# A two-block transformer stack on one core: the attention bias written to DRAM as single rows and copied there from ScalarE's queue, and every third attention pair a banded one

## The chip, the cores and the metric

The kernel runs on one core of one Trainium2 chip. The metric is the device time of one execution in microseconds (us). Before the change the median of three runs is 2673.74 us (2669.78 to 2679.16). The profile is of one further execution.

The engines are named as the profile names them: PE is TensorE's matmul, PEld its weight load, DVE is VectorE, ACT is ScalarE, POOL is GpSimd and SP is SyncE. SPq and ACTq are the queues from which SP and ACT issue DMAs. An engine takes its instructions strictly in order, and a DMA issue is one of them.

## What is computed

One sequence of 512 tokens of width 1024 goes through a first block of two layers and then a second block of two layers. The change touches only the first block. Each of its layers is, in short:

```python
h = rms_norm(x, g_pre)
a_q, a_kv, a_g, b_cq, b_ckv, b_kr, c_q, c_kv, z = split_cols(h @ w_in)
# 4 heads, each with three branches: compressed keys, all blocks, window 512
o_a = g[..., 0] * o_cmp + g[..., 1] * o_slc + g[..., 2] * o_win
# 4 heads of causal attention over up-projected queries and keys (96 wide)
o_b = causal_block_attention(q_full, k_full, v, (64 + 32) ** -0.5)
# 8 heads, window 128, with a sink logit in the softmax
o_c = banded_attention(c_q, c_k, c_v, 128, rel_bias[4:], sinks)
mixed = concatenate([o_a, o_b, o_c]) * silu(z)
x = x + rms_norm(mixed @ w_out, g_post)
```

The first four and the last eight heads add a relative bias to their logits: `rel_bias[head, t5_bucket(query - key)]`. It depends on the distance alone, so for a head it is one row over all distances, and a tile of 128 queries needs that row shifted by one position from partition to partition. `rel_bias` is the same in both layers. The second block (a pooling and gated-recurrence mixer between two feed-forward parts, per layer) is the larger part of the time, and its code is the same before and after.

## The kernel before

Everything is kept with 128 features on the partitions and 512 tokens in a row. A dense product is done in float32 by three passes on PE: each weight tile (128 x 1024, 512 KB) is split on DVE into a high part (`one_hi`) and the rest (`one_lo`), and so are the activations (`xh`, `xl`). The weight tiles of the first block come through `fetch_first` from SP's queue into a ring of four raw buffers. The next fetch into a buffer waits until its tile is split. Per layer there are 24 tiles of `w_in` (function `attend`, loop over `i` in `tensor`, line 1036) and 8 of `w_out` (`project_out`).

PE writes the products of `w_in` into six PSUM banks in turn. DVE evicts them (`evict`, line 779) and multiplies by `xrstd`, the reciprocal root of the mean square of x, which ACT makes (lines 702 and 705) once PE has summed the squares (line 1048). So tile 6 can't start before the first eviction. DVE does the split of tile i + 2 ahead of the evictions of round i, in one order written out by hand. At round 10 DVE reads `s1`, a block of small weights that ACT's queue fetches (line 699).

The bias is made at the start of layer 0. PE multiplies `rel` by a one-hot matrix `hot` after its first two weight tiles (`distance_rows`, line 556), DVE adds a mask (`mask_rows`, line 565), and the results are `vec` (4 x 1024, one row for each of the four heads) and `near` (8 x 384). Two DMAs on SP's queue, after the fetch of tile 7, write each row 128 times to DRAM (`store_bias`, line 526): `far_bias` is 4 x 128 x 1024 (2048 KB) and `near_bias` 8 x 128 x 384 (1536 KB). After the fetch of tile 11 two more DMAs on SP's queue wait for both stores and read the shifted tiles `biasA` and `biasC` back (`read_bias`, line 532).

The attention is a list of 48 pairs (`attention_pairs`, line 348). A pair is two heads of one kind for one block of 128 queries: 24 of the three branches (cmp, slc, win), then 8 causal ones (mla), then 16 banded ones (swa). A pair goes through five stages on four engines, and the engines work on different pairs at the same time. At step j:

- PE multiplies queries by keys for pair j (line 959), transposes the probabilities of pair j - 3 (line 973) and multiplies those of pair j - 4 by the values (line 987);
- DVE adds the bias to the logits and takes the maximum (line 825), takes the reciprocals of the sums of pair j - 1 (line 799), and makes a third of the copies of the transposed probabilities (line 839);
- ACT takes the exponentials and their sums (line 764) and makes the other copies (line 773);
- POOL scales the probabilities (lines 665 and 666), both heads of a pair, but only the first head where the pair has over two key blocks (DVE then does the second).

Each of the eight output tiles has one of two PSUM banks, in turn; DVE multiplies a finished one by silu(z) (line 812). ACT and POOL turn the finished tiles into `xh` and `xl` for `w_out` (lines 751 and 1129).

Of the kernel before, what the change touches and what calls it, by code (L numbers as in the profile page):

```python
# [459 lines left out]
class First:  # L460


    def __init__(self, kit, ctx):
# [19 lines left out]
        with ExitStack() as early:  # L483
# [26 lines left out]
def start_engines(kit, first):  # L510
# [21 lines left out]
    def read_bias(sp):  # L532

        sp.wait_ge(s["stored"], 32)
        for dst, name, sem, heads, w, n in ((kit.biasC, "near", "read_c", C_HEADS, NEAR_W, 256),
                                            (kit.biasA, "far", "read_a", A_HEADS, 2 * T, BIAS_W)):
# [18 lines left out]

    def distance_rows(pe):
        pe.wait_ge(s["loaded"], 80)
# [3 lines left out]
        pe.wait_ge(s["vec_made"], 1)  # L561
        pe.matmul(bank[5][0:C_HEADS, 0:NEAR_W], first.rel[:, A_HEADS:], first.hot[:, 256:256 + NEAR_W],
                  start=True, stop=True).then_inc(s["vec_mm"], 1)

    def mask_rows(v):
        v.wait_ge(s["loaded"], 80)
        for i in range(2):
# [4 lines left out]
        v.tensor_tensor(first.near[:], bank[5][0:C_HEADS, 0:NEAR_W], first.msk_near[:], ALU.add  # L572
                        ).then_inc(s["vec_made"], 1)

    return dict(sync=sync, store_bias=store_bias, read_bias=read_bias, scalar=scalar, vector=vector, tensor=tensor,
                distance_rows=distance_rows, mask_rows=mask_rows)


def attend(kit, first, l, begin):
# [99 lines left out]
    def sync(sp):  # L679
        for n in range(max(n0, RAW_RING), n0 + st.per_layer):  # L680
            sp.wait_ge(st.w_split, n + 1)
            fetch_first(sp, st, n)
# [4 lines left out]

    def scalar(a):
# [1773 lines left out]
```

## Time and profile before

| | us |
|---|---|
| median of three runs | 2673.74 |
| the profiled execution | 2676.89 |
| its span on the core | 2674.8 |
| PE busy in the span | 2472.3 (92%) |
| DVE busy | 1294.3 (48%) |
| ACT busy | 661.5 (25%) |
| POOL busy | 654.8 (24%) |

The busy shares are means over stages with different limits. The page's row of 40 slices shows PE at 7 tenths in the first slice and 0 in the second (66.87 us each), and at 7 to 9 in all others. In the second slice PE's granted clock is at 5 tenths. The span less the profiled execution's own time is 2.1 us, which lies outside all that is told here.

### The profile page before, as it was taken

To read this page: it belongs to the slowest core of one execution; us is meant where nothing else is said; L and a number is where in the kernel's file an instruction comes from. 1 tells how busy PE (TensorE), PEld (TensorE's weight loads), DVE (VectorE), ACT (ScalarE), POOL (GpSimd) and SP (SyncE) were. 2 spreads that over 40 slices of the span, in tenths; PEclk is the share of its full clock that TensorE was granted. 3 is DMA by queue.
4 is the path that set the end of the run, shared out by engine and by line. 5 is a ranking of instruction groups with operands and counts; after the bars stand their busy time and mean duration, and the time that the engine had idled before them with its cause. 6 is when DMAs were issued, how large, how long until landed. Compare 5 with 4: busy or idle time off the path is not lost. (4 is left out here: it accounts for less than half of the span.)

```text
span 2674.8 us, 35071 instructions
## 1 busy us (share of the span) xinstructions
PE 2472.3 (92%) x13238; PEld 1985.8 (74%) x13238; DVE 1294.3 (48%) x1920; ACT 661.5 (25%) x1329; POOL 654.8 (24%) x510
## 2 busy tenths in 40 slices
PE   7089999999789999999899999899999998999997
PEld 5066677866668888788688888788888787788886
DVE  4045656557453334586643334433343776533344
ACT  3001643037121110253321110311100643311101
POOL 1000561016333331200333321233311101433311
PEclk9589999999989999998999999999999998999999
DMA  5341013200033332221223232223322221223322
GB/s 166 56 139 47 17 48 126 86 25 17 16 117 98 98 109 93 71 98 41 79 87 101 94 117 92 64 94 98 107 98 83 95 65 56 79 95 101 111 99 78
DMA packets 58641, 224.79 MB, mean 84 GB/s; under 512 B 6392, under 2 KB 8576, under 8 KB 58276
## 3 DMA queue, kind: packets, MB, share of 16 engines
q1 hardware_dynamic: 57380, 215.49, 25.3%
q10 hardware_dynamic: 1152, 7.78, 0.8%
q8 instruction: 77, 1.26, 0.2%
q14 instruction: 32, 0.26, 0.0%
HBM read 217.47 MB, written 5.77 MB: 83 GB/s over the span
## 5 line engine op out<-in xcount | busy, mean ns | idle before, releaser
L172 DVE CAST two_hi<-two_raw 128x1024 fp32r<-128x1024 f32 (+1 forms) x292 | 219.8, 753 | 908.0 <-PE bank L241 896.5
L234 PE MATMUL bank<-xh,two_hi 128*128 128x512 f32 x1728 | 429.6, 391 | 0.0
L241 PE MATMUL bank<-xl,two_hi 128*128 128x512 f32 x1728 | 427.5, 389 | 0.0
L237 PE MATMUL bank<-xh,two_lo 128*128 128x512 f32 x1728 | 426.9, 389 | 0.0
L174 DVE TENSOR_TENSOR two_lo<-two_raw,two_hi 128x1024 fp32r<-128x1024 f32 (+1 forms) x292 | 401.0, 1373 | 10.0
L237 PEld LDWEIGHTS bank<-xh,two_lo 128*128 128x128 f32 x1728 | 324.3, 188 | 67.5
L241 PEld LDWEIGHTS bank<-xl,two_hi 128*128 128x128 f32 x1728 | 324.3, 188 | 67.4
L234 PEld LDWEIGHTS bank<-xh,two_hi 128*128 128x128 f32 x1728 | 323.0, 188 | 68.2 <-issue 1.1
L1579 POOL TENSOR_TENSOR up_hm<-up_sg,up_hm 128x512 f32<-128x512 f32 x88 | 197.6, 2245 | 556.4 <-ACT up_hm L1561 556.4
L449 PE MATMUL bank<-xh,one_hi 128*128 128x512 f32 x448 | 122.5, 418 | 81.0 <-DVE one_hi L172 81.0
L234 PE MATMUL bank<-hh,two_hi 128*128 128x512 f32 x704 | 171.8, 392 | 0.0
L172 DVE CAST one_hi<-one_raw 128x1024 fp32r<-128x1024 f32 x64 | 45.5, 710 | 260.6 <-PE bank L456 134.8
L241 PE MATMUL bank<-hl,two_hi 128*128 128x512 f32 x704 | 171.4, 390 | 0.0
L237 PE MATMUL bank<-hh,two_lo 128*128 128x512 f32 x704 | 170.0, 389 | 0.0
L449 PEld LDWEIGHTS bank<-xh,one_hi 128*128 128x128 f32 x448 | 88.0, 198 | 104.8 <-issue 86.0
L1561 ACT ACTIVATE up_hm<-bank 128x512 f32<-128x512 f32 x88 | 52.9, 601 | 416.5 <-PE bank L241 413.7
L665 POOL TENSOR_SCALAR lg_ring<-lg_ring,inv,gate 128x31 f32<-128x31 f32 (+4 forms) x80 | 45.0, 570 | 450.6 <-DVE inv L799 450.3
L234 PEld LDWEIGHTS bank<-hh,two_hi 128*128 128x128 f32 x704 | 132.1, 188 | 29.3 <-issue 1.9
L237 PEld LDWEIGHTS bank<-hh,two_lo 128*128 128x128 f32 x704 | 132.1, 188 | 27.5
L241 PEld LDWEIGHTS bank<-hl,two_hi 128*128 128x128 f32 x704 | 132.2, 188 | 27.3
L1582 POOL TENSOR_TENSOR hl<-up_hm,hh 128x512 f32 x88 | 115.1, 1308 | 83.7 <-ACT hh L1563 83.7
L453 PE MATMUL bank<-xh,one_lo 128*128 128x512 f32 x448 | 112.7, 394 | 0.0
(289 smaller groups left out, 2923.2 us busy)
## 6 DMA issues: line engine op xcount, KB each, us to landing
two_raw<-in_up SPq DMA_DIRECT2D x180, 512.0 KB, 3.4
two_raw<-in_down SPq DMA_DIRECT2D x64, 704.0 KB, 4.0
one_raw<-in_w_in SPq DMA_DIRECT2D x48, 512.0 KB, 3.5
two_raw<-in_w_in SPq DMA_DIRECT2D x40, 512.0 KB, 3.4
one_raw<-in_w_out SPq DMA_DIRECT2D x16, 512.0 KB, 3.4
two_raw<-in_w_out SPq DMA_DIRECT2D x16, 512.0 KB, 4.1
w<-in_w ACTq DMA_DIRECT2D x2, 2048.0 KB, 11.6
x<-in_x SPq DMA_DIRECT2D x4, 512.0 KB, 6.9
```

The source lines that it names most:

```text
L172: v.tensor_copy(st.hi[:, h, 0:w], st.raw[:, r, 0:w]).then_inc(st.hi_made, 1)
L174: v.tensor_tensor(st.lo[:, h, 0:w], st.raw[:, r, 0:w], st.hi[:, h, 0:w].bitcast(F32), ALU.subtract).then_inc(st.w_split, 1)
L234: pe.matmul(out[:], st.hi[:, slot, k * P:(k + 1) * P], xh[:, h * kp + k, :], start=h == 0 and k == 0, stop=False)
L237: pe.matmul(out[:], st.lo[:, slot, k * P:(k + 1) * P], xh[:, h * kp + k, :], start=False, stop=False)
L241: mm = pe.matmul(out[:], st.hi[:, slot, k * P:(k + 1) * P], xl[:, h * kp + k, :], start=False, stop=h == pieces - 1 and k == kp - 1)
L449: pe.matmul(out[:], st.hi[:, slot, w * P:(w + 1) * P], xh[:, k, :], start=k == 0, stop=False)
L453: pe.matmul(out[:], st.lo[:, slot, w * P:(w + 1) * P], xh[:, k, :], start=False, stop=False)
L665: return eng.tensor_scalar(row, row, inv[:, i, hh:hh + 1], gate[:, u["n"], b:b + 1], ALU.mult, ALU.mult)
L1561: a.activation(hm[:, f, :], bank[1][:], ACT.Copy).then_inc(s["out_taken"], 1)
L1579: g.tensor_tensor(hm[:, f, :], sg[:, f, :], hm[:, f, :], ALU.mult).then_inc(s["h_made"], 1)
L1582: g.tensor_tensor(hl[:, at, :].rearrange("p o t -> p (o t)"), hm[:, f, :], hh[:, at, :].rearrange("p o t -> p (o t)").bitcast(F32), ALU.su ...
```

## The change

It has two parts.

The bias: the four small inputs (`rel`, `hot`, `msk`, `msk_near`) are fetched first of all on SP's queue. The one-hot products become PE's first instructions and the mask DVE's first after its memsets, and the last of the three products goes to a bank of its own. SP's queue stores only `vec` and `near` themselves, as 4 and 8 rows, and then fetches `k1`, which had been among the first. ACT's queue then copies each row 128 times from DRAM to DRAM (`copy_bias`), ahead of its fetches of `s1` and `w1`, and reads the shifted tiles back (`read_bias`) after the last of the eight Silu of layer 0. The reads by DVE of `biasA` and `biasC` are the same.

The attention: the list of pairs is made of triples, two from the old list without the banded ones and then one banded pair. So two output tiles are open at a time, the banded tiles mostly in bank 7 and the others mostly in bank 4. The tiles finish in the order 4, 0, 5, 1, 6, 2, 3, 7, and `w_out` takes them in that order.

```diff
@@ attention_pairs
+    others, banded = [u for u in pairs if u["kind"] != "swa"], [u for u in pairs if u["kind"] == "swa"]
+    pairs = [u for k in range(len(banded)) for u in (others[2 * k], others[2 * k + 1], banded[k])]
@@
-N_NSA, N_MLA = 24, 8
 SPLIT_AT = (17, 20)
-TILES = (0, 1, 2, 3, 4, 5, 6, 7)
+TILES = (4, 0, 5, 1, 6, 2, 3, 7)
...
+OUT_BANKS = (7, 4, 7, 4, 7, 4, 4, 7)
@@ start_engines
     def sync(sp):
+        for dst, src in ((first.rel, "rel"), (first.hot, "hot"), (first.msk, "msk"), (first.msk_near, "msk_near")):
+            sp.dma_start(dst[:], d[src]).then_inc(s["loaded"], 16)
         sp.dma_start(kit.gains[:], d["gains"]).then_inc(s["gains_in"], 16)
...
-        for dst, src in ((first.rel, "rel"), (first.hot, "hot"), (first.msk, "msk"), (first.msk_near, "msk_near"),
-                         (kit.k1, "k1")):
-            sp.dma_start(dst[:], d[src]).then_inc(s["loaded"], 16)
         for n in (2, 3):
             fetch_first(sp, st, n)
-
-    def store_bias(sp):
         sp.wait_ge(s["vec_made"], 3)
-        sp.dma_start(d["far"], first.vec[0:A_HEADS].unsqueeze(1).to_broadcast([A_HEADS, P, 2 * T])
-                     ).then_inc(s["stored"], 16)
-        sp.dma_start(d["near"], first.near[:].unsqueeze(1).to_broadcast([C_HEADS, P, NEAR_W])).then_inc(s["stored"], 16)
...
+        sp.dma_start(d["far_row"], first.vec[:]).then_inc(s["stored"], 16)
+        sp.dma_start(d["near_row"], first.near[:]).then_inc(s["stored"], 16)
+        sp.dma_start(kit.k1[:], d["k1"]).then_inc(s["k1_in"], 16)
+
+    spread = (("near", "read_c", kit.biasC, C_HEADS, NEAR_W, 256), ("far", "read_a", kit.biasA, A_HEADS, 2 * T, BIAS_W))
+
+    def copy_bias(a):
+
+        a.wait_ge(s["stored"], 32)
+        for name, _, _, heads, w, _ in spread:
+            row = d[f"{name}_row"]
+            a.dma_start(d[name], bass.AP(row.tensor, row.offset, [[w, heads], [0, P], [1, w]])).then_inc(s["copied"], 16)
+
+    def read_bias(a):
+
+        a.wait_ge(s["copied"], 32)
+        for name, sem, dst, heads, w, n in spread:
             src = d[name]
...
+        mask_rows(v)
 
     def tensor(pe):
         pe.sem_inc(st.mm_done, HL_RING)
         pe.wait_ge(s["set"], 3)
-
-    def distance_rows(pe):
-        pe.wait_ge(s["loaded"], 80)
+        pe.wait_ge(s["loaded"], 64)
         for i in range(2):
             pe.matmul(bank[(5, 3)[i]][0:A_HEADS, :], first.rel[:, 0:A_HEADS], first.hot[:, i * T:(i + 1) * T],
                       start=True, stop=True).then_inc(s["vec_mm"], 1)
-        pe.wait_ge(s["vec_made"], 1)
-        pe.matmul(bank[5][0:C_HEADS, 0:NEAR_W], first.rel[:, A_HEADS:], first.hot[:, 256:256 + NEAR_W],
+        pe.matmul(bank[7][0:C_HEADS, 0:NEAR_W], first.rel[:, A_HEADS:], first.hot[:, 256:256 + NEAR_W],
                   start=True, stop=True).then_inc(s["vec_mm"], 1)
@@ attend: sync
-            if n == 7:
-                begin["store_bias"](sp)
-            if n == 11:
-                begin["read_bias"](sp)
@@ attend: scalar
+        if l == 0:
+            begin["copy_bias"](a)
         a.dma_start(s1[:], d["s1"][l]).then_inc(s["s1_in"], 16)
         a.dma_start(w1[:], d["w1"][l]).then_inc(s["w1_in"], 16)
...
             a.activation(proj[:, C_Z + c, :], proj[:, C_Z + c, :], ACT.Silu).then_inc(s["z_made"], 1)
+            if l == 0 and c == DC - 1:
+                begin["read_bias"](a)
...
-        convert_at = {NU - 4: (0, 1), NU - 3: (2, 3), NU - 2: (4,), NU: (5,), NU + 1: (6,)}
+        convert_at = {}
+        for p in range(DC - 1):
+            at = max(NU - L_RING + p // 2 + TURN_LAG + 1, last_of[TILES[p]] + WEIGH_LAG + 2, *convert_at)
+            convert_at.setdefault(at, []).append(p)
@@ attend: vector, step
-                if x == NU - 1 or pairs[x + 1]["tile"] != pairs[x]["tile"]:
-                    tile = pairs[x]["tile"]
+                tile = pairs[x]["tile"]
+                if x == last_of[tile]:
@@ attend: tensor, weigh
-            order = TILES.index(tile)
-            if order >= 2:
-                pe.wait_ge(s["mixed"], order - 1)
+            ahead = [p for p in range(TILES.index(tile)) if OUT_BANKS[p] == out_bank[tile]]
+            if ahead:
+                pe.wait_ge(s["mixed"], ahead[-1] + 1)
```

What stands on SP's queue around the stores before; "waits" names the semaphore that holds an instruction back:

```order
L345 DMA one_raw<-in_w_in 128x1024 [waits one_w_split] x4
L528 DMA far_bias<-vec 512x1x1024 [waits start_vec_made]
L530 DMA near_bias<-near 1024x1x384
L345 DMA one_raw<-in_w_in 128x1024 [waits one_w_split] x4
L538 DMA biasC<-near_bias 128x8x256 [waits start_stored]
L538 DMA biasA<-far_bias 128x4x896
L345 DMA one_raw<-in_w_in 128x1024 [waits one_w_split] x12
```

And now, on the same queue:

```order
L521 DMA x<-in_x 128x1024 x2
L345 DMA one_raw<-in_w_in 128x1024 x2
L527 DMA far_bias_row<-vec 4x1024 [waits start_vec_made]
L528 DMA near_bias_row<-near 8x384
L529 DMA k<-in_k 128x1281
L345 DMA one_raw<-in_w_in 128x1024 [waits one_w_split] x20
```

The two wide stores and the two reads have left the queue of the weight fetches; two stores of 4 and 8 rows and the fetch of `k1` stand there instead, before tile 4.

What stands on ACT between the squares of x and the first Silu before (`s` is `s1`, `w` is `w1`, `proj` holds the projections):

```order
L698 ACTIVATE proj<-x 128x512 x8
L699 DMA s<-in_s 128x1835
L700 DMA w<-in_w 128x4096
L702 ACTIVATE xrstd<-bank,eps 128x512 [waits first0_xsq_summed]
L705 ACTIVATE xrstd<-xrstd 128x512 [waits first0_ln_made]
```

And now, on to the reads:

```order
L702 ACTIVATE proj<-x 128x512 x8
L538 DMA near_bias<-near_bias_row 1024x1x384 [waits start_stored]
L538 DMA far_bias<-far_bias_row 512x1x1024
L705 DMA s<-in_s 128x1835
L706 DMA w<-in_w 128x4096
L708 ACTIVATE xrstd<-bank,eps 128x512 [waits first0_xsq_summed]
L711 ACTIVATE xrstd<-xrstd 128x512 [waits first0_ln_made]
L712 ACT_TABLE_LOAD
L715 ACTIVATE proj<-proj 128x512 [waits first0_taken] x8
L545 DMA biasC<-near_bias 128x8x256 [waits start_copied]
L545 DMA biasA<-far_bias 128x4x896
```

The two copies now stand ahead of `s1`, `w1` and the two steps that make `xrstd`, and they wait for the row stores.

What POOL scales at the end of the causal pairs and in the banded ones before (`lg_ring` holds the probabilities, `inv` the reciprocals; 128x256 and 128x128 here are one head of a banded pair, 128x512 and 128x384 of a causal one):

```order
L666 TENSOR_SCALAR lg_ring<-lg_ring,inv 128x512
L666 TENSOR_SCALAR lg_ring<-lg_ring,inv 128x384
L666 TENSOR_SCALAR lg_ring<-lg_ring,inv 128x256 x2
L666 TENSOR_SCALAR lg_ring<-lg_ring,inv 128x128 x2
L666 TENSOR_SCALAR lg_ring<-lg_ring,inv 128x256 x6
```

And now, from the first pair on (lines with `gate` are the pairs of the three branches):

```order
L673 TENSOR_SCALAR lg_ring<-lg_ring,inv,gate 128x31 x2
L673 TENSOR_SCALAR lg_ring<-lg_ring,inv,gate 128x512
L674 TENSOR_SCALAR lg_ring<-lg_ring,inv 128x256 x2
L673 TENSOR_SCALAR lg_ring<-lg_ring,inv,gate 128x512
L673 TENSOR_SCALAR lg_ring<-lg_ring,inv,gate 128x31 x2
L674 TENSOR_SCALAR lg_ring<-lg_ring,inv 128x256 x2
```

The banded pairs no longer stand in one run at the end; each has two other pairs before it.

## Rows read from the trace of the kernel before

**Rows 1.** Timeline at PE's long wait: start, duration, engine, instruction, [idle before <-releaser].

```profile
62.81 1.97 PE L456 MATMUL bank<-xl,one_hi 128*128 128x512 f32 x8
...
144.92 0.69 DVE L172 CAST one_hi<-one_raw 128x1024 fp32r<-128x1024 f32 x1 [88.36 <-DMA one_raw<-in_w_in]
...
145.76 3.75 PE L449 MATMUL bank<-xh,one_hi 128*128 128x512 f32 x8 [80.98 <-DVE one_hi L172]
...
152.87 1.77 PEld L449 LDWEIGHTS bank<-xh,one_hi 128*128 128x128 f32 x8
```

**Rows 2.** Timeline of SP's queue, 30 to 144 us.

```profile
30.00 0.78 SPq L528 DMA_DIRECT2D far_bias<-vec  x1
30.82 34.25 SPq L530 DMA_DIRECT2D near_bias<-near  x1
...
65.11 56.72 SPq L345 DMA_DIRECT2D one_raw<-in_w_in  x1
...
143.66 0.39 SPq L538 DMA_DIRECT2D biasC<-near_bias  x1
```

**Rows 3.** DMA view, 40 to 50 us: the queue's packets, MB, share of 16 engines.

```profile
q1 hardware_dynamic: 64, 0.26, 24.5%
```

**Rows 4.** DMA view, 65 to 80 us.

```profile
q1 hardware_dynamic: 335, 0.76, 45.7%
```

**Rows 5.** DMA view, 2660 to 2675 us, the final store of x from 128 partitions.

```profile
GB/s 0 0 0 0 0 0 0 0 0 0 0 0 0 339 415 404 240 0 164 415 404 404 11 0 0 0 426 415 393 164 0 0 0 262 426 415 295 0 0 0
```

**Rows 6.** Timeline of PE around the one-hot products.

```profile
25.53 1.88 PE L559 MATMUL bank<-hot,rel 32*4 32x512 f32 x4
...
29.31 3.14 PE L449 MATMUL bank<-xh,one_hi 128*128 128x512 f32 x8
...
36.51 1.98 PE L449 MATMUL bank<-xh,one_hi 128*128 128x512 f32 x8
38.33 1.98 PE L453 MATMUL bank<-xh,one_lo 128*128 128x512 f32 x8
```

**Rows 7.** Timeline of the first 7 us: the small fetches and the first split.

```profile
4.33 0.74 SPq L522 DMA_DIRECT2D rel<-in_rel  x1
...
6.10 0.27 SPq L522 DMA_DIRECT2D msk_near<-in_msk_near  x1
...
6.67 0.69 DVE L172 CAST one_hi<-one_raw 128x1024 fp32r<-128x1024 f32 x1 [5.49 <-DMA one_raw<-in_w_in]
```

**Rows 8.** Busy time by stretch: us, PE, PEld, DVE, ACT, POOL (instructions), PEclk, DMA share, GB/s.

```profile
0.00:20.00 20.00, 7.67 (x25) 5.79 (x26) 6.98 (x7) 15.49 (x25) 12.89 (x12) 1.00 0.90 323
80.00:100.00 20.00, 0.00 (x0) 0.00 (x0) 0.00 (x0) 0.00 (x0) 0.00 (x0) 0.50 0.42 46
```

**Rows 9.** Timeline: xrstd on ACT, and DVE's first use of s1.

```profile
43.01 0.69 ACT L702 ACTIVATE xrstd<-bank,eps 128x512 f32<-128x512 f32 x1 [23.05 <-PE bank L1048]
...
166.72 0.16 DVE L875 TENSOR_SCALAR nsink<-s 128x8 f32<-128x8 f32 x1
```

**Rows 10.** Layer 0's attention by stretch (columns of rows 8).

```profile
263.19:309.87 46.68, 42.47 (x357) 25.89 (x356) 32.16 (x142) 31.77 (x115) 21.60 (x38) 0.97 0.07 24
309.87:328.30 18.43, 18.36 (x131) 12.15 (x130) 13.44 (x51) 12.09 (x39) 11.86 (x12) 1.00 0.01 2
328.30:354.60 26.30, 25.70 (x234) 16.21 (x233) 20.04 (x100) 20.38 (x70) 23.45 (x30) 1.00 0.01 2
354.60:362.50 7.90, 6.09 (x47) 4.03 (x47) 2.26 (x8) 5.34 (x16) 7.88 (x9) 0.78 0.00 0
```

**Rows 11.** POOL's groups by form, 328 to 359 us: count, busy, mean ns, idle before.

```profile
L666 POOL TENSOR_SCALAR lg_ring<-lg_ring,inv 128x256 f32<-128x256 f32 x25 | 22.8, 925 | 2.1 <-DVE inv L799 2.0
L666 POOL TENSOR_SCALAR lg_ring<-lg_ring,inv 128x128 f32<-128x128 f32 x10 | 5.9, 606 | 0.8 <-DVE inv L799 0.8
```

**Rows 12.** DVE's reads of the maxima (one for each head), layer 0 and layer 1.

```profile
L825 DVE DVE_READ_ACCUMULATOR2_ANT negm<- x96: 71/83/86, 263.3 to 355.2; 128x1 f32 x96
...
L825 DVE DVE_READ_ACCUMULATOR2_ANT negm<- x96: 71/83/86, 577.7 to 669.1; 128x1 f32 x96
```

More of the change, by code:

```diff
@@ L519, in sync @@
                 fetch_first(sp, st, i)
-        for dst, src in ((first.rel, "rel"), (first.hot, "hot"), (first.msk, "msk"), (first.msk_near, "msk_near"),
-                         (kit.k1, "k1")):
-            sp.dma_start(dst[:], d[src]).then_inc(s["loaded"], 16)
         for n in (2, 3):
             fetch_first(sp, st, n)
-    def store_bias(sp):
         sp.wait_ge(s["vec_made"], 3)
-        sp.dma_start(d["far"], first.vec[0:A_HEADS].unsqueeze(1).to_broadcast([A_HEADS, P, 2 * T])
-                     ).then_inc(s["stored"], 16)
-        sp.dma_start(d["near"], first.near[:].unsqueeze(1).to_broadcast([C_HEADS, P, NEAR_W])).then_inc(s["stored"], 16)
[L532 to L536, printed above, removed]
+        sp.dma_start(d["far_row"], first.vec[:]).then_inc(s["stored"], 16)
[10 more added lines that the diff above has]
+        for name, sem, dst, heads, w, n in spread:
             src = d[name]
-            sp.dma_start(dst[:], bass.AP(src.tensor, src.offset + P - 1, [[w - 1, P], [w * P, heads], [1, n]])
-                         ).then_inc(s[sem], 16)
+            a.dma_start(dst[:], bass.AP(src.tensor, src.offset + P - 1, [[w - 1, P], [w * P, heads], [1, n]])
+                        ).then_inc(s[sem], 16)
     def scalar(a):
@@ L571, in mask_rows @@
         v.wait_ge(s["vec_mm"], 3)
-        v.tensor_tensor(first.near[:], bank[5][0:C_HEADS, 0:NEAR_W], first.msk_near[:], ALU.add
+        v.tensor_tensor(first.near[:], bank[7][0:C_HEADS, 0:NEAR_W], first.msk_near[:], ALU.add
                         ).then_inc(s["vec_made"], 1)
-    return dict(sync=sync, store_bias=store_bias, read_bias=read_bias, scalar=scalar, vector=vector, tensor=tensor,
-                distance_rows=distance_rows, mask_rows=mask_rows)
+    return dict(sync=sync, copy_bias=copy_bias, read_bias=read_bias, scalar=scalar, vector=vector, tensor=tensor)
 def attend(kit, first, l, begin):
@@ L606, in attend @@
     turn_bank = [(3, 6)[g % 2] for g in range(len(groups))]
-    out_bank = {t: (4, 7)[i % 2] for i, t in enumerate(TILES)}
+    out_bank = {t: OUT_BANKS[i] for i, t in enumerate(TILES)}
+    last_of = {u["tile"]: i for i, u in enumerate(pairs)}
+    first_of = {kind: min(i for i, u in enumerate(pairs) if u["kind"] == kind) for kind in ("cmp", "mla", "swa")}
+    n_swa = [sum(u["kind"] == "swa" for u in pairs[:i + 1]) for i in range(NU)]
+    assert list(TILES) == sorted(TILES, key=last_of.get)
     def here(j):
@@ L773, in scalar @@
                         a.activation(dst, src, ACT.Copy).then_inc(s["pt_by_a"], 1)
-            for p in convert_at.get(j, ()):
+            for p in convert_at.pop(j, ()):
+                convert(p)
+        for late in convert_at.values():
+            for p in late:
                 convert(p)
@@ L880, in vector @@
                     v.wait_ge(start["stored"], 32)
+                    v.wait_ge(start["k1_in"], 16)
                 v.tensor_tensor(rot_k[:, 0, :], proj[64:96, C_KR, :], cos, ALU.mult).then_inc(s["rot_made"], 1)
@@ L934, in vector @@
         v.wait_ge(s["z_made"], DC)
-        v.wait_ge(start["read_a"], 16)
         for j in range(NU + WEIGH_LAG + 1):
-            if j == N_NSA + N_MLA:
+            if j == first_of["cmp"]:
+                v.wait_ge(start["read_a"], 16)
+            if j == first_of["swa"]:
                 v.wait_ge(start["read_c"], 16)
@@ L995, in step @@
                     pe.wait_ge(s["logits"], 2 * (i - 1))
[L996 to L998 removed]
+                if i == first_of["mla"]:
                     pe.wait_ge(s["qk_made"], 2 * B_HEADS)
                     pe.wait_ge(s["uk_kept"], B_HEADS)
+                if i == first_of["cmp"]:
+                    pe.wait_ge(s["kc_made"], 2)
                 for hh in range(2):
@@ L1050, in tensor @@
             if i == 12:
+                if l == 0:
+                    pe.wait_ge(start["k1_in"], 16)
                 pe.wait_ge(s["taken"], C_KR + 1)
@@ L2446, in program @@
     dram["far"] = nc.dram_tensor("far_bias", (A_HEADS, P, 2 * T), F32, kind="Internal").ap()
+    for kind, heads, w in (("far", A_HEADS, 2 * T), ("near", C_HEADS, NEAR_W)):
+        dram[f"{kind}_row"] = nc.dram_tensor(f"{kind}_bias_row", (heads, w), F32, kind="Internal").ap()
     dram["near"] = nc.dram_tensor("near_bias", (C_HEADS, P, NEAR_W), F32, kind="Internal").ap()
```

15 lines of the change are left out of this document (4 added, 11 removed).

## Prediction, made before the changed kernel ran

> **What bounds the kernel now.** I read the page's slices first: PE is the busiest engine everywhere, except that slice 2 of 40 shows it idle. The timeline of that slice shows one hole. PE ends a tile of `w_in` (tile 7) at about 64.4 us and starts tile 8 at 145.7 [rows 1]. The row names the split as its releaser, and the split's own row names the DMA of the weights, for which DVE had idled 88.36 us. Then I read SP's queue backwards [rows 2]: the fetch of tile 8 was issued at 65.11, because the issue of the `near` store before it had taken 34.25 us; its own issue took 56.72 us, and the queue's next step that waits for both stores passed at 143.66. So two stores of 3.5 MB hold the weight stream for 81 us. Elsewhere in the first block PE is nearly dense, except in the attention: there PE, DVE, ACT and POOL all have gaps, and in the banded stretch POOL is busy 23.45 of 26.30 us, in the tail after the last logits 7.88 of 7.90 [rows 10].
>
> **Why the stores are slow.** From 40 to 50 us the queue moves 0.26 MB with a 24.5% share of 16 DMA engines: four engines, all their time, 26 GB/s together [rows 3]. Once `near` runs beside it, 45.7%, so between seven and eight engines, and 51 GB/s [rows 4]. At the end of the kernel the same kind of transfer, SBUF to DRAM, but from 128 partitions, moves up to 426 GB/s [rows 5], 26.6 GB/s an engine. So writing DRAM isn't what is slow; four engines read four partitions at the pace of one. Two things could do that: few engines, and a shared way out of few partitions. The change takes away only the second, since its copies have the same shape (4 or 8 rows, each 128 times).
>
> **The bias, step by step.**
>
> *The hole.* PE idles 81.0 us [rows 1]. After it a tile takes 152.87 - 145.73 = 7.14 us; a steady one takes 3 x (38.33 - 36.51) = 5.46 [rows 6]. That is 1.7 us of lower clock. Both go, 82.7 us, if tiles 8 and on are fetched in time. In that case SP's queue holds nothing but fetches, which have four buffers of 5.46 us each ahead.
>
> *The one-hot products leave the middle.* PE leaves the dense products at 25.5 and returns at 29.31, and the tile after it again takes 36.51 - 29.31 = 7.20 us. Without both, tile 3 starts at 25.5 + 5.5 = 31.0 in place of 36.5: 5.5 us gained.
>
> *They come first instead.* Four issues on SP's queue, from 4.33 to 6.37 us [rows 7], 2.0 us, now stand ahead of x and the weights, so the first split moves from 6.67 to about 8.7. PE's products and DVE's masks take from 25.5 to about 30.0 in the old place, with 1.2 us of waiting for a shared bank; now they would start near 4.7, when the small inputs have landed, and DVE would be through near 8.2, under the wait for the first weights. I cost them at the 2.0 us of the queue; if the small inputs land 1 us later, 1 us more. Net of the start: 3.5 us gained.
>
> *The copies.* The row stores come behind 4 MB of x and weights. The first 20 us move 323 GB/s [rows 8], so I put their landing at 17 us. At 26.6 GB/s an engine, `far` is 128 x 4096 bytes on each of four engines, 19.7 us, and `near` 128 x 1536 on each of eight, 7.4 us. Together they end at 17 + 27 = 44 us. The bias is first read in the attention, at about 175 us, and the reads themselves (2.8 MB, behind the last Silu) pass beside the dense products as they did before. So the copies cost nothing by themselves. No row shows a copy from DRAM to DRAM; its bounds are 426 GB/s (all engines, 8 us) and the old pace (26 to 51 GB/s, 105 us). I take the pace of an engine from rows 5.
>
> *What waits behind them on ACT.* ACT is an engine here: an issue that doesn't return holds the step after it. In rows 2 the third transfer's issue returned only when much of the one before was through (34.25 of the 79 us that `far` takes at 26 GB/s, 0.43). By that, ACT is free of its issues at 17 + 7.4 + 0.43 x 19.7 = 33 us. It needs to be free when PE has the sum of squares, 43.01 [rows 9] less 3.5, so at 39.5. Six us to spare, and some 6 more before PE, which has six banks, would stop. `s1` lands behind the copies near 50; DVE reads it at 166.72 - 86 = 81. Nothing is added.
>
> Sum for the bias: 82.7 + 3.5 = 86.2 us.
>
> The Trainium skill has a rule against this part (DMA: Bandwidth & Descriptors, Why a DMA increments its semaphore by 16 and not by 1): a DMA uses the largest number of engines up to 16 that divides the slowest dimension of both sides, so these copies still run on 4 and 8. The trace agrees for the stores (24.5% and 45.7% of 16 engines). A reader who expects 16 engines would have the copies end at 25 us, not 44; the sum is the same by both.
>
> **The attention.** The work is the same: 48 pairs, the same operations, and DVE's share of the copies is 8448 columns for 8576. What moves is when. Layer 0 takes 99.3 us: 24 pairs of branches at 1.95 us each, 8 causal at 2.30, 16 banded at 1.64, and a tail of 7.9 [rows 10]. In the banded stretch POOL's need is 24 x 0.925 + 8 x 0.606 = 27.0 us [rows 11] for a stretch of 26.3, and what is left over runs on into the tail. Spread over all 48 pairs POOL has 61 us in 91. What is late next: in the banded stretch PE shows 25.70 busy of 26.30, DVE and ACT 20.0 and 20.4. PE's ends are modelled, so its true need lies between PEld's 16.2 and that 25.7. If a banded pair goes at 1.5 us instead of 1.64, that is 2.3 us; and the tail, with POOL's backlog gone and the clock not at 0.78, may give 1.7. I take 4 us a layer. Far ends: banded pairs at the pace of DVE and ACT (1.27), the tail 3 shorter, and PE's 4.2 idle us among the branches gone, 13 us; or banded pairs slowed to 1.95 by wide neighbours, 5 us lost. The new waits are for the banks: a tile's first product with values waits for DVE's product two open tiles before it; that is due one or two steps ahead in the hand-written order, so nothing. PE's start on `w_out` now waits for the tile finished last but one instead of four pairs before the end, at most one 0.69 us product. Layer 1 has the same stretch (91.4 for 91.9 us between first and last maxima [rows 12]), so 8 us in all, between -10 and +26.
>
> **Sum.** 86.2 + 8 = 94 us off the profiled execution's 2676.9: 2583. That execution stands 3 us above the median of the runs shown; against the median the sum gives 2580. I forecast 2582.
>
> **Rivals.**
>
> 1. *The copies are as slow as the stores were*: the limit was the number of engines or the write side. For it: same shape, same engines. Against it: rows 5, where an engine writes DRAM at 26.6 GB/s, four times the pace in rows 3. Then `near` ends at 17 + 27 = 44 and ACT's issues return at 44 + 34 = 78; `xrstd` is made at 80 in place of 41, DVE's splits of tiles 6 and on stand behind its evictions, and PE stops at tile 6, due near 48, until about 84: 36 us. `s1` lands near 126, some 5 us late for round 10 of the delayed stream. 41 us lost: 2582 + 41 = 2623.
> 2. *The interleaving gives nothing*, since a pair's chain over four engines, not POOL, sets the pace: 2590; with the loss of 5 us a layer 2600.
> 3. *The interleaving frees all four engines*: 13 us a layer, 2564.
> 4. *Slower than before*: the same place as rival 1, but the copies reading one DRAM row 128 times over go at a third less than even the old pace. They would end near 175, `s1` with them, and DVE's read of it at round 10 (due 81) would hold the splits of all later tiles: over 94 us lost, 2677 and more. It decides from a copy time of about 158 us, against 105 in the old form and 27 in my sum. Nothing in the rows speaks for it.
> 5. *The change doesn't do what it says*: the weight stream still stalls behind the row stores. They are 28 KB, and the fetches around them have four buffers; not more than a few us.
>
> **How the numbers follow.** Forecast (copies fast, 1 to 8 us a layer) 0.52; rival 2 0.18; rival 3 0.14; rival 1, or a copy slow enough to delay `xrstd` by 5 us or more, 0.13; rival 4 0.02; the rest 0.01 around no change. The range reaches from rival 3 to a mild form of rival 1: 2562 to 2610, which leaves out most of rival 1 and rival 4. A change under 0.3% (8 us) can't be told from none here. Faster by more than that 0.97, within it 0.01, slower 0.02.
>
> **What would show it.** Right: no wait of PE above a few us before 175 us, and the first logits near 177 instead of 263; SP's fetches issued without a long duration; ACT's issues of the two copies and `s1` over by about 35 us and `xrstd` made by 41; POOL busy about two thirds throughout the attention, and the attention 95 us instead of 99.3. Wrong: an issue on ACT's queue of over 20 us, with `xrstd` late and PE idle at tile 6 (rival 1); a wait of DVE for `s1` at round 10 (rival 4); or an attention of 99 us or more with PE waiting for POOL or DVE as before (rival 2).

## The result, and the profile after

| | us |
|---|---|
| before, median of 4 runs | 2676.45 (2669.78 to 2680.52) |
| after, median of 4 runs | 2601.98 (2599.66 to 2604.04) |
| ratio | 0.9724, 95% interval 0.9700 to 0.9748 |
| profiled execution after, its span | 2600.92, 2599.0 |

The time fell by 74.5 us. The forecast was 2582, so 94. The two parts of the change went opposite ways: the bias part did what its sum said, and the attention, forecast 4 us a layer shorter, became over 5 us a layer longer.

**The hole.** PE's timeline answers to [rows 1]. Columns, as in all timelines: start, duration, engine, instruction.

```profile
61.50 1.98 PE L458 MATMUL bank<-xl,one_hi 128*128 128x512 f32 x8
63.31 1.98 PE L451 MATMUL bank<-xh,one_hi 128*128 128x512 f32 x8
...
68.53 1.77 PEld L451 LDWEIGHTS bank<-xh,one_hi 128*128 128x128 f32 x8
```

Tile 8 starts at 63.31 without a wait. The weight load of tile 9 starts at 68.53, where it started at 152.87 [rows 1]: 84.3 us earlier.

**The copies.** First the two queues from 9 to 42 us, answering to [rows 2, 7, 9], then DMA from 20 to 30 us (GB/s in 40 slices; packets, MB, share of 16 engines):

```profile
9.26 0.55 DVE L577 TENSOR_TENSOR near<-bank,msk_near 8x384 f32<-8x384 f32 x1 [0.60 <-PE bank L567]
9.74 0.67 DVE L172 CAST one_hi<-one_raw 128x1024 fp32r<-128x1024 f32 x1
9.84 0.27 SPq L527 DMA_DIRECT2D far_bias_row<-vec  x1
...
16.16 1.25 ACTq L538 DMA_DIRECT2D near_bias<-near_bias_row  x1
17.44 4.52 ACTq L538 DMA_DIRECT2D far_bias<-far_bias_row  x1
22.00 16.18 ACTq L705 DMA_DIRECT2D s<-in_s  x1
...
38.21 1.21 ACTq L706 DMA_DIRECT2D w<-in_w  x1
...
41.70 0.69 ACT L708 ACTIVATE xrstd<-bank,eps 128x512 f32<-128x512 f32 x1 [20.51 <-PE bank L1060]
```

```profile
GB/s 205 172 205 184 209 209 197 203 203 203 197 203 197 197 197 203 209 203 197 209 203 197 197 203 197 197 197 209 209 176 123 107 106 106 117 82 115 115 98 115
...
q10 hardware_dynamic: 1052, 1.75, 45.8%
```

`near` moves at some 200 GB/s on eight engines (45.8% of 16 is 7.3), `far` then at some 105 on four: 25 and 26 GB/s an engine, as [rows 5] had it. The issue of `s1` took 16.18 us, the only long one. ACT is free at 39.4 and makes `xrstd` at 41.70, right behind PE's sum of squares. Nothing was lost, but only 2.3 us were to spare.

**The attention.** The windows of layer 0 answer to [rows 10]: pairs 0 to 17, 18 to 35, 36 to 47 by DVE's first row of each, the tail, and two stretches of 8 us within the second (us, PE, PEld, DVE, ACT, POOL, PEclk, DMA share, GB/s). Then DVE's reads of the maxima in both layers, which answer to [rows 12], and POOL's two banded forms over the whole attention, which answer to [rows 11].

```profile
177.03:211.23 34.20, 30.82 (x266) 18.67 (x262) 23.83 (x110) 23.41 (x84) 19.51 (x30) 1.00 0.01 2
211.23:250.10 38.87, 33.35 (x267) 20.91 (x266) 24.33 (x112) 23.88 (x87) 20.78 (x32) 0.91 0.09 28
250.10:275.90 25.80, 24.54 (x187) 16.00 (x186) 17.66 (x71) 18.72 (x59) 18.02 (x18) 1.00 0.01 1
275.90:281.56 5.66, 4.78 (x50) 3.12 (x49) 2.29 (x9) 3.15 (x11) 4.66 (x6) 1.00 0.01 3
217.00:225.00 8.00, 4.74 (x30) 3.32 (x30) 5.10 (x20) 4.09 (x15) 3.39 (x5) 0.70 0.19 67
225.00:233.00 8.00, 7.78 (x66) 4.73 (x64) 4.15 (x16) 3.66 (x12) 2.04 (x3) 0.87 0.01 2
```

```profile
L839 DVE DVE_READ_ACCUMULATOR2_ANT negm<- x96: 70/83/86, 177.2 to 276.5; 128x1 f32 x96
...
L839 DVE DVE_READ_ACCUMULATOR2_ANT negm<- x96: 71/82/88, 495.2 to 594.2; 128x1 f32 x96
```

```profile
L674 POOL TENSOR_SCALAR lg_ring<-lg_ring,inv 128x256 f32<-128x256 f32 x28 | 25.6, 928 | 13.3 <-DVE inv L813 13.2
L674 POOL TENSOR_SCALAR lg_ring<-lg_ring,inv 128x128 f32<-128x128 f32 x12 | 7.1, 603 | 9.7 <-DVE inv L813 9.7
```

POOL does wait now: 23 us before these two forms, where the same ones of before waited 2.9 in the banded run [rows 11]. PE did not profit. First to last maxima take 99.3 and 99.0 us for 91.9 and 91.4; the tail is 2.2 us shorter (5.7 for 7.9). From DVE's first bias row at 177.03 (263.19 before) the attention lasts 104.5 us, 5.2 longer, and in layer 1 it is 5.4 longer.

The timeline where DVE has pair 21 and PE transposes pair 18 has the largest piece:

```profile
215.15 0.68 DVE L853 COPY pt_ring<-bank 128x512 f32<-128x512 f32 x1
...
215.75 0.68 DVE L172 CAST one_hi<-one_raw 128x1024 fp32r<-128x1024 f32 x1
...
216.46 1.22 DVE L174 TENSOR_TENSOR one_lo<-one_raw,one_hi 128x1024 fp32r<-128x1024 f32 x1
...
217.60 0.68 DVE L826 TENSOR_TENSOR proj<-bank,proj 128x512 f32<-128x512 f32 x1
...
218.20 0.68 DVE L839 CUSTOM_DVE_ANT_0 lg_ring<-bank,biasA 128x512 f32<-128x512 f32 x1
...
218.93 0.72 ACT L775 ACTIVATE lg_ring<-lg_ring,negm 128x512 f32<-128x512 f32 x1 [3.57 <-DVE negm L839]
...
219.68 1.90 POOL L674 TENSOR_SCALAR lg_ring<-lg_ring,inv 128x256 f32<-128x256 f32 x2 [3.89 <-DVE inv L813]
...
220.85 1.08 PE L987 MATMUL bank<-k,lg_ring 128*128 128x128 f32 x4 [3.26 <-ACT pt_ring L784]
```

The split of a `w_out` tile (at step 20, as `SPLIT_AT` has it in both kernels) now stands in one row with a wide copy, the product of a finished tile and the bias of a 512-wide pair. DVE has no gap there, ACT waits 3.57 us, POOL 3.89, PE 3.26. During PE's wait its granted clock falls from 1.00 to 0.50, the lower of its two levels (1.2 GHz): 0.80 is the mean over 219 to 221 us, then it is 0.50 to 227 us and 0.99 over 227 to 229.

### The profile page after: what moved, and what is told of

The parts are those of the page before. It is cut to its first block and busy times, and to the rows that moved or that the text cites. A ratio compares the mean times of both kernels' runs of the same rounds, so it can differ in the third digit from the quotient of the medians.

```text
span 2599.0 us, 35078 instructions
## 1 busy us (share of the span) xinstructions
PE 2473.8 (95%) x13238; PEld 1984.4 (76%) x13238; DVE 1295.9 (50%) x1920; ACT 661.9 (25%) x1329; POOL 653.8 (25%) x510
## 3 DMA queue, kind: packets, MB, share of 16 engines
q1 hardware_dynamic: 54288, 208.96, 24.4%
## 5 line engine op out<-in xcount | busy, mean ns | idle before, releaser
L451 PE MATMUL bank<-xh,one_hi 128*128 128x512 f32 x448 | 117.0, 404 | 0.0
L458 PE MATMUL bank<-xl,one_hi 128*128 128x512 f32 x448 | 110.7, 389 | 0.0
```

The lines of the kernel that those rows point to most:

```text
L451: pe.matmul(out[:], st.hi[:, slot, w * P:(w + 1) * P], xh[:, k, :], start=k == 0, stop=False)
L458: mm = pe.matmul(out[:], st.hi[:, slot, w * P:(w + 1) * P], xl[:, k, :], start=False, stop=k == DC - 1)
```

## The experiments

A median stands beside the runs of the kernel before in its own batch (2675.5, 2679.0, 2675.0). Times of one kernel lie within some 10 us, often in two clusters 7 us apart, so a difference of two medians under 5 us says little, and I then read the profiles. "Body" is PE's first to last logits of a layer, "tail" from there to the first product of `w_out`. "Idle" is the body less the time that PE is busy in it. "Low" is the time of the body in which PE's granted clock is 0.50, added up from windows of 2 us. All are us, layer 0 / layer 1:

| kernel | median | ratio, 95% | body 0 / 1 | tail 0 / 1 | idle | low |
|---|---|---|---|---|---|---|
| before | 2676.5 | | 91.9 / 91.1 | 8.2 / 8.2 | 4.9 / 5.6 | 3.2 / 0 |
| after | 2602.0 | 0.9700 to 0.9748 | 99.1 / 98.9 | 6.0 / 5.9 | 10.2 / 10.2 | 6.8 / 6.8 |
| e1 bias only | 2586.8 | 0.9649 to 0.9688 | 91.9 / 90.7 | 8.2 / 8.3 | 4.7 / 5.3 | 3.4 / 0 |
| e2 order only | 2687.0 | 1.0029 to 1.0064 | 99.2 / 101.7 | 5.9 / 5.9 | 10.2 / 9.7 | 6.8 / 13.7 |
| e3 splits early | 2592.2 | 0.9666 to 0.9701 | 96.5 / 96.6 | 5.9 / 6.0 | 8.6 / 7.7 | 3.4 / 6.8 |
| e4 splits late | 2593.4 | 0.9677 to 0.9707 | 99.2 / 96.7 | 6.0 / 5.9 | 7.4 / 8.7 | 13.4 / 3.4 |
| e5 copies from SBUF | 2659.0 | 0.9910 to 0.9959 | 99.0 / 100.3 | 5.9 / 5.9 | 10.1 / 8.8 | 6.8 / 13.6 |
| e6 e3, copies placed | 2590.9 | 0.9663 to 0.9703 | 97.9 / 94.2 | 5.3 / 5.4 | 7.3 / 8.3 | 10.2 / 0 |
| e7 e1, masks behind splits | 2589.4 | 0.9650 to 0.9686 | 93.0 / 90.8 | 6.9 / 8.1 | 4.7 / 5.3 | 6.8 / 0 |
| e8 e3, longer lags | 2593.1 | 0.9661 to 0.9701 | 93.8 / 94.8 | 7.9 / 7.9 | 7.2 / 6.8 | 6.8 / 10.3 |
| e9 e7, longer lags | 2592.6 | 0.9677 to 0.9710 | 96.1 / 95.9 | 6.8 / 6.8 | 8.6 / 8.6 | 6.8 / 6.9 |
| e10 e6, longer lags | 2589.2 | 0.9668 to 0.9699 | 91.8 / 93.9 | 7.7 / 7.7 | 8.2 / 7.4 | 0 / 6.8 |
| e11 e7, DVE scales banded | 2584.5 | 0.9646 to 0.9678 | 93.4 / 92.3 | 8.1 / 6.8 | 5.0 / 5.2 | 6.8 / 3.3 |

The last two columns say what a body is made of. Dense work takes up to twice as long at half the clock, so x us of low clock cost about x / 2 (an estimate). After against e1, the body is 7.2 and 8.2 us longer: 5.5 and 4.9 more idle time, and 1.7 and 3.4 by the clock. The low stretches move about between executions even where the code is the same: e4 has 13 us of them at the start of layer 0, after has none there, and the two differ only from step 17 on. So a difference of bodies under some 4 us is read with these columns beside it.

**Each part alone.** e1 takes the order of pairs, `TILES`, the banks and `convert_at` of before; e2 takes before and only these of after.

```diff
-    others, banded = [u for u in pairs if u["kind"] != "swa"], [u for u in pairs if u["kind"] == "swa"]
-    pairs = [u for k in range(len(banded)) for u in (others[2 * k], others[2 * k + 1], banded[k])]
...
-TILES = (4, 0, 5, 1, 6, 2, 3, 7)
+TILES = (0, 1, 2, 3, 4, 5, 6, 7)
...
```

> The changed kernel with the old list of pairs, old tile order and banks and old places of the conversions; the bias part stays. Theory A (the bias part gains 86 us, the interleaving loses 5 us a layer): 86 us less than before, so about 2590, and 10 to 11 us less than the changed kernel; the attention takes 99.3 and 98.8 us again, the first logits come near 177 us. Rival (the slower attention of the changed kernel comes from the bias part, for example from where bias tiles or weights land): the attention stays at 104 us and the time near 2601.

> The kernel before with the new list of pairs, tile order, banks and places of the conversions alone; the bias is stored and read as before. Theory A: 10 to 11 us slower than before, 2687; attention 104 us in both layers with a PE wait of 3.3 us at pair 18 in each. Rival (interleaving needs the early bias to pay, or its loss is bound to the bias part): same as before within 3 us.

The bias part alone gives 88.7 us, the order alone costs 11.5. Both are within 4 us of their expectations. The profile of e2 has the same wait of PE, 3.3 us at its longest, in both layers. Its layer 1 is 2.5 us longer than the 99.2 us of layer 0, with twice the low clock.

**The splits moved.** e3 has them at steps 12 and 14, e4 at 31 and 33:

```diff
-SPLIT_AT = (17, 20)
+SPLIT_AT = (12, 14)
```

> The changed kernel with DVE's two splits of w_out tiles behind steps 12 and 14 of the attention instead of 17 and 20, so that neither stands ahead of a tile's product with silu(z) or of a 512-wide pair. Theory A (the loss is one place: split, tile product and wide pair in a row on DVE, PE idle 3.26 us, then its clock at 0.7): the wait and the low clock at pair 18 to 24 go, the attention takes 99 to 100 us, the kernel 4 to 6 us less a layer, 2591 to 2593. Rival B (the interleaved order is slower all along, because banded pairs stretch the chain of wide ones): the wait moves, the attention stays within 1 us of 104.4 a layer.

> As the early-split kernel, but with the splits behind steps 31 and 33, among pairs of one key block. Theory A: the same gain, 4 to 6 us a layer, unless the fetch of the next w_out tiles, which waits for these splits, comes too late for w_out (then a PE wait at w_out's tile 2 or 3). Rival B: within 1 us of 104.4 a layer.

By the medians they give back 9.8 and 8.6 us, as theory A had it. Body and tail together don't come down to its 99 to 100 us: they are 102.4 and 102.6 us in e3, 105.2 and 102.6 in e4. PE's waits over 170 to 380 us, in e3 and then in e1 (engine, line, releaser: us, times, longest), and e3's window that answers to the first 8 us above:

```profile
PE bank L987 <- ACT pt_ring L784: 3.5, 7, 1.0
PE bank L1001 <- ACT pt_ring L784: 2.6, 4, 1.0
```

```profile
PE bank L982 <- ACT pt_ring L779: 1.4, 3, 0.5
...
PE bank L996 <- ACT pt_ring L779: 1.0, 2, 0.6
```

```profile
217.00:225.00 8.00, 6.90 (x62) 4.28 (x62) 5.63 (x21) 5.22 (x20) 4.42 (x6) 1.00 0.01 2
```

The wait of 3.26 is gone (the longest is 1.0 in e3 and in e4). So is the low clock behind it, but for 3.4 us in layer 1 of e4. Over both layers PE's idle time falls by 4.1 us in e3 and by 4.3 in e4, of the 10.4 that the interleaving had added (after against e1). So the one place is shown for about two fifths of the added idle time, and for a low clock behind it that costs about 3 us a layer. The medians put it at 9 to 10 of 15 us, but they also hold the clock of the rest of the run: e4's layer 0 is as long as after's, with less idle time and twice the low clock. The rest is spread: PE waits 7.5 us for ACT's copies in layer 0 of after, 6.1 in e3 and 2.4 in e1.

**Which property of the source made the stores slow.** e5 is after, but the copies read SBUF:

```diff
-        a.wait_ge(s["stored"], 32)
-        for name, _, _, heads, w, _ in spread:
-            row = d[f"{name}_row"]
-            a.dma_start(d[name], bass.AP(row.tensor, row.offset, [[w, heads], [0, P], [1, w]])).then_inc(s["copied"], 16)
+        a.wait_ge(s["vec_made"], 3)
+        for dst, row, heads, w in ((d["near"], first.near[:], C_HEADS, NEAR_W),
+                                   (d["far"], first.vec[0:A_HEADS], A_HEADS, 2 * T)):
+            a.dma_start(dst, row.unsqueeze(1).to_broadcast([heads, P, w])).then_inc(s["copied"], 16)
```

> The changed kernel, but the two wide copies on ACT's queue read vec and near in SBUF (4 and 8 partitions, each 128 times), not the rows in DRAM. Same place, same queue, same shapes, same 4 and 8 DMA engines; only the source differs. Theory (the stores were slow because few partitions share one way out, my prediction's): near takes about 27 us and far up to 79 again, ACT's issues return near 78 instead of 39.4, xrstd is made near 80 instead of 41.7, PE stops at tile 6 for about 36 us: 2602 + 36 = 2638, range 2625 to 2650. Rival 1 of the prediction (the number of engines or the write side was the limit, and being off the weights' queue is all that helped): the copies go as fast from SBUF as from DRAM, no wait of PE, 2602 within 5.

It measured 2659.0: 57 us lost, where the expectation had 36 and at most 48. ACT's queue; then DMA from 20 to 28 us (mostly `near`), and from 55 to 65 (`far`):

```profile
16.43 13.20 ACTq L538 DMA_DIRECT2D far_bias<-vec  x1
29.67 52.24 ACTq L705 DMA_DIRECT2D s<-in_s  x1
81.95 4.96 ACTq L706 DMA_DIRECT2D w<-in_w  x1
86.95 0.69 ACT L708 ACTIVATE xrstd<-bank,eps 128x512 f32<-128x512 f32 x1 [65.27 <-issue]
```

```profile
q10 hardware_dynamic: 267, 0.41, 44.9%
```

```profile
q10 hardware_dynamic: 62, 0.25, 22.7%
```

The share of engines is the same as from DRAM (`near` 44.9% against 45.8%, `far` 22.7% against 25.5% over 30 to 33 us), the speed a quarter: 0.41 MB in 8 us is 51 GB/s, 0.25 in 10 is 25. Shape, queue and destination are the same, so the source in SBUF sets it, and rival 1's reason (number of engines, write side) falls. That it is the few partitions is argued and not shown. From 4 to 8 rows the engines double with the partitions, at 6.4 GB/s an engine each time. So an engine slowed by reading one SBUF row over and over would look the same; no run has few rows on more partitions. `xrstd` is made 45 us later. The first logits stand at 228.8 for 176.5, and PE's two waits (48.6 us) explain most of it:

```profile
91.64 1.62 PE L451 MATMUL bank<-xh,one_hi 128*128 128x512 f32 x3 [40.34 <-DVE one_hi L172]
```

```profile
141.28 3.75 PE L451 MATMUL bank<-xh,one_hi 128*128 128x512 f32 x8 [8.24 <-DVE one_hi L172]
```

```profile
136.28 0.17 DVE L887 TENSOR_SCALAR nsink<-s 128x8 f32<-128x8 f32 x1 [7.64 <-DMA s<-in_s]
```

That is the place and the second step (`s1` late at round 10) that rival 1 described; it priced them at 41 us. After both waits PE's clock is lower for a while (0.78 and 0.71).

**What is left of the interleaving's loss.** e6 gives DVE one group of each wide pair, and 8 of the narrow ones; e8 lengthens the lags:

```diff
-    copied_by_v = [g % 3 == 0 for g in range(len(groups))]
+    copied_by_v, narrow = [], 0
+    for i, heads in groups:
+        if pairs[i]["m"] > 2:
+            copied_by_v.append(heads == (0,))
+        else:
+            copied_by_v.append(narrow % 9 in (1, 5))
+            narrow += 1
```

```diff
-TURN_LAG, WEIGH_LAG = 3, 4
+TURN_LAG, WEIGH_LAG = 4, 5
```

> The interleaved kernel with its two weight splits at steps 12 and 14 (2592.2), and DVE's third of the copies placed otherwise: one of the two groups of each wide pair (12), and 8 of the 36 narrow groups, in place of every third group. The columns that DVE copies are the same, 8448. Theory P (what is left of the interleaving's loss, about 2.5 us a layer, is the waits of PE for ACT's copies, 3.5 + 2.4 us in layer 0's attention against 1.4 + 0.6, where both groups of a wide pair fell to ACT): those waits fall to about 2 us and the attention from 101.6 to about 99; 2587 to 2589. Theory S (the heavy and the light pairs next to each other cost it whoever copies): 2592 within 3.

> The interleaved kernel with its splits at steps 12 and 14 (2592.2), and PE transposes pair j - 4 and multiplies pair j - 5 by the values, instead of j - 3 and j - 4: one more step between DVE's bias and maximum and PE's use of it. Theory C (what sets the pace is the chain of a pair over DVE, ACT, POOL and PE, rival 2 of the prediction): the waits at L987 and L1001 go, the body of the attention falls from 96.4 to about 92 a layer, the tail grows by 1: 2584 to 2587. Theory S (the work of each step, in strict order on each engine, sets the pace; a longer chain changes nothing): 2592 to 2595, the longer tail only.

> The interleaved kernel with all three mends: splits at steps 12 and 14, DVE's copies one group of each wide pair, lags 4 and 5. Singly: splits 2592.2, with the copies placed 2590.9, with the lags 2593.1. If the waits they take away are different ones, the body falls to 92 or less a layer (old order 91.8 and 91.0) and the tail stands at 8: 100 a layer, 2587 to 2589. If they are the same waits, 94 and 8: 2591 to 2593. Even the best case gives no more than the old order: interleaving saves nothing that POOL's backlog had cost.

The totals can't be told apart (2589 to 2593), and the 2584 to 2587 of theory C did not come. The lags take 2.7 and 1.8 us off the body, and 2.0 returns as tail, as one more step has to drain. PE's idle time in the body falls by only 1.4 and 0.9 us; the rest of the gain is a pair's work that has moved into the tail. So theory C is right for a small part: pairs do wait for each other there. e6's two layers went in opposite directions (+1.4, -2.4), and so did the low clock (+6.8, -6.8), so it settles nothing. With both (e10) the body is 91.8 and 93.9, but PE's idle time is 8.2 and 7.4 against 4.7 and 5.3 in the old order. What that remainder waits for is not shown by any of them.

> Bias part with masks behind splits, old order of the pairs (2589.4; in its profile 93.0 us from first to last logits of layer 0 and 6.9 on to w_out), and the transposes and value products one step later (j - 4 and j - 5). In the interleaved kernel this took 2.7 and 1.8 us off the body and put 2.0 on the tail of each layer. Theory C (the chain of a pair is too short in either order): the body falls by 2 to 3 us here too, the tail grows by 2, 2588 to 2591. Theory O (the old order had no such wait, it is the interleaving that makes neighbours unlike and needs slack): the body stays at 91 to 93, the tail grows by 2 a layer, 2592 to 2594.

In the old order the same lags lengthen the body, by 3.1 and 5.1 us, and the tail doesn't grow. Neither theory had that. PE's idle time rises by 3.9 and 3.3 us, and layer 1 also has 6.9 us of low clock that e7 had not. The old order did not need the slack; why it loses stays open.

**Was POOL the bound?** e11 takes 8 of POOL's 32 banded heads a layer to DVE:

```diff
-    scaled_by_v = [[hh == 1 and u["m"] > 2 for hh in range(2)] for u in pairs]
+    scaled_by_v = [[hh == 1 and (u["m"] > 2 or u["kind"] == "swa" and i % 2 == 0) for hh in range(2)]
+                   for i, u in enumerate(pairs)]
```

> Bias part with masks behind splits, old order of the pairs (2589.4), and DVE scales the second head of every second banded pair (8 of 32 heads a layer), which POOL did at 925 or 606 ns each. It tests the premise of the interleaving, that POOL sets the pace of the banded run (23.93 busy of 26.50 us, then 7.47 of 7.50 in the tail). If POOL does: POOL's need in the two falls by 7 us, the run from 26.5 to about 23 and the tail by 1 to 2: 4 to 5 us a layer, 2579 to 2582. If it is PE (25.70 busy of 26.50) or the chain: the run stays at 26, 2587 to 2590, or 1 us a layer more for DVE's 2.5 us.

The windows of the banded run and the tail, in e7 and then in e11:

```profile
242.00:268.50 26.50, 25.70 (x232) 16.13 (x230) 20.07 (x100) 21.16 (x73) 23.93 (x30) 1.00 0.01 2
268.50:276.00 7.50, 5.90 (x50) 4.21 (x51) 2.32 (x5) 5.07 (x14) 7.47 (x9) 1.00 0.00 0
```

```profile
242.00:268.50 26.50, 25.50 (x232) 16.17 (x232) 21.87 (x106) 20.53 (x71) 17.73 (x22) 1.00 0.01 2
268.50:276.00 7.50, 5.70 (x46) 3.91 (x44) 2.41 (x9) 5.11 (x16) 7.00 (x8) 0.77 0.00 0
```

POOL's need in the run falls from 23.93 to 17.73 us and PE does the same 232 matmuls in the same 26.5 us. So POOL did not set the pace of the banded run. What did is PE, 25.70 and 25.50 us busy, or something that leaves no gap in its row. In the tail POOL is still 7.00 of 7.50 busy, 4.98 of it with the conversion for `w_out`. The length of the old order's tail goes with the clock in it and not with POOL's load: 8.1 to 8.3 us where it is low (0.77 in e11, 0.78 in [rows 10]), 6.8 or 6.9 where it is 1.00. The median, 2584.5, lies within e7's runs (2581.0 to 2589.9).

**The start.** e7 is e1 with two moves:

```diff
         v.memset(kit.ones[:], 1.0).then_inc(s["set"], 1)
-        mask_rows(v)
...
+        a.dma_start(s1[:], d["s1"][l]).then_inc(s["s1_in"], 16)
+        a.dma_start(w1[:], d["w1"][l]).then_inc(s["w1_in"], 16)
         if l == 0:
             begin["copy_bias"](a)
-        a.dma_start(s1[:], d["s1"][l]).then_inc(s["s1_in"], 16)
-        a.dma_start(w1[:], d["w1"][l]).then_inc(s["w1_in"], 16)
...
             for i in range(HL_RING):
                 split(i)
+            begin["mask_rows"](v)
```

> The bias part alone (old order of the pairs, 2586.8), with two moves: DVE adds the three masks behind its splits of tiles 0 and 1 instead of ahead of them, and ACT issues s1 and w1 ahead of the two copies. PE's one-hot products stay first. Expected if the start is bound by DVE's masks: the first split at about 8.7 instead of 9.7, 1 us gained, 2585 to 2586; the row stores 3 us later; ACT's issues free within 30 us or at 42 at the latest, xrstd still at 41 to 43. If instead the first weights land only at 9.7, nothing: 2587 within 2. If the copies' own issue, now last, still blocks for 16 us behind w1: xrstd near 45, up to 3 us lost, 2590.

```profile
8.10 0.69 DVE L172 CAST one_hi<-one_raw 128x1024 fp32r<-128x1024 f32 x1 [6.93 <-DMA one_raw<-in_w_in]
```

```profile
15.03 0.38 ACTq L701 DMA_DIRECT2D s<-in_s  x1
15.45 0.52 ACTq L702 DMA_DIRECT2D w<-in_w  x1
...
23.30 1.25 ACTq L536 DMA_DIRECT2D near_bias<-near_bias_row  x1
24.58 5.41 ACTq L536 DMA_DIRECT2D far_bias<-far_bias_row  x1
...
39.65 0.69 ACT L706 ACTIVATE xrstd<-bank,eps 128x512 f32<-128x512 f32 x1 [18.04 <-PE bank L1056]
```

The first split starts at 8.10, for 9.64 in e1, and tile 3 at 33.15 for 34.02. So the masks did hold the start, by 0.9 us at tile 3. The first logits stand at 174.4 for 176.9 in e1, but 1.7 of these 2.5 us are a stretch of low clock in e1 from 128 to 136 us (0.63 and 0.94) that e7 hasn't. ACT's issues are over at 30.0 instead of 39.4, with none over 5.41 us. The 0.9 us are shown by the profile alone; the medians (2589.4 and 2586.8) don't resolve them.

**A version that beats both** is e1, with or without the moves of e7 and e11: 2584 to 2589, against 2602 and 2676.

## Why the prediction was right and wrong

*The hole* was 82.7 in the sum and is 83.0 (84.3 by tile 9, less the 1.3 of the start). Right.

*The start* was 3.5 and is 1.3: tile 3 starts at 35.21, not 36.51. The failed step was "DVE would be through near 8.2, under the wait for the first weights". Its last mask ends at 9.8, because the first four products take 3.57 us where they took 1.88 [rows 6], and the first weights had landed by 8.10 (e7). So 3.07 us were lost ahead of the split, not 2.0. The remaining 1.1 us are in PE's pace after it: its products come 0.43 us apart until about 22 us and then 0.23. In e1, with the same start, they come 0.23 apart from 19.9, and tile 3 starts at 34.02. So they belong to the execution. That holds for the old start too: e2 has it, and its tile 3 starts at 39.53, not 36.51.

*The bias sum* of 86.2 came out at 85.9 (PE's first logits at 176.47 for 262.41), but not by its own steps: most of the 2.2 missing at the start is made good by 1.6 between tile 9 and the attention that I had not counted. PE idles 2.79 us in either. Before, its clock was 0.91 on the mean from 210 to 230 us, which is 3.4 us at 0.50 and cost about 1.7; after has no such stretch. I can't tie that to the change, and e1 has one, so this part of the agreement is luck.

*The copies* went at the pace of an engine in rows 5, as the sum had it, as long as few other transfers ran beside them. The Trainium skill (DMA: Bandwidth & Descriptors, The descriptor swizzle) assigns partitions 0 to 3 to one port and 4 to 7 to another in a transfer to 128 partitions. The trace fits that: in e5 four rows move at 25 GB/s, eight at 51. It would be the "shared way out of few partitions" that the prediction supposed, but no run tells it from a slow repeated read of SBUF. The 8 and 4 engines held for DRAM and SBUF sources alike.

*ACT's issues* were to be free at 33 and were at 39.4. The rule drawn from one issue of before (0.43 of `far`) held: when the issue of `s1` returned at 38.2, `far` had moved 0.9 of its 2.1 MB, and in e5 at 81.9 it had moved 0.8. The times put into the rule were short. `near` was through at 27.5, not 24.4; the 0.43 of `far` took 10.7 us, not 8.5, since weights moved beside it; and the issue of `w1` added 1.2. It cost nothing, with 2.3 us to spare where I had said six. In e5 the same kind of issue (52.24 us) cost 40 us.

*The attention* was forecast at -8 and is +10.7: 18.7 of the 20 us by which the forecast missed. Two steps of it failed. The first was "what is left over runs on into the tail", with POOL as the limit of the banded run: e11 takes POOL away and the run stays. I had both readings of [rows 10] in hand (POOL 23.45, PE 25.70 of 26.30) and took the one that the change served, because PE's ends are modelled. The second was that moved instructions cost nothing where they land. The prediction looked at new waits for banks and at POOL, but not at what DVE has in a row at each step. Its far end of a loss, 5 us a layer, was right by size. The "wide neighbours" of a banded pair that it gave as the reason are not what was found: about two fifths of the added idle time, and the low clock behind it, is the fixed step of a split that now meets a tile's product and a 512-wide pair (e3, e4). The rest stays open. The tail was forecast 1.7 us shorter and is 2.2, of which about 1.3 is the clock, since the old tail lasts 6.9 us where its clock isn't low (e7).

Of the rivals, number 2 with its loss (2600) is what happened; the range held the time because of it, and the forecast itself had the sign of the attention wrong. Its reason, a pair's chain over four engines, is borne out for 2.3 us of idle time in the two layers (e8).

## What to carry to other kernels

When the order of units is changed, fixed positions in the program (a split at step 17 or 20) are part of the change: lay out what one in-order engine has in a row at each of them, and move them too. An engine that is busy nine tenths of a stretch is not yet its limit when another one is too; give a quarter of its work away before redesigning the order around it. For a broadcast from few partitions to DRAM, write the rows once and copy them from there. And before two profiles are compared by the length of a stage, take apart how much of it is idle time and how much is low clock.

## What the runs showed of the hardware

- A transfer of 4 or 8 rows read 128 times goes at 25 or 51 GB/s from as many partitions of SBUF, and at 105 or 200 GB/s from DRAM, on the same 4 or 8 engines (e5 against after).
- An issue behind a wide transfer holds its engine until some four tenths of `far` have moved: 34.25 us before (26 GB/s for 34.25 us is 0.9 of 2.1 MB), 52.24 in e5 (0.8 MB), 16.18 in after (0.9 MB). The same issue placed ahead of them takes 0.38 (e7).
- In all six layers in which PE waits 3.3 us in mid-attention (after, e2, e5) its granted clock goes to 0.50 for some 6.8 us behind the wait; so the wait costs about 3 us more than itself. A low clock also comes without such a wait, as at the start of layer 0 in e4.
